# Prompt scores of a stick-breaking attention layer as three one-pass products of split queries and keys, and a cache ring of two places instead of three

## What is computed

```python
def sb_logits(q, k, sb_bias):
    z = jnp.einsum('bqhd,bkhd->bhqk', q, k).astype(jnp.float32) * SB_SCALE
    return z + sb_bias.astype(jnp.float32)[None, :, None, None]
# 8 heads x 64; prompt: strictly causal over 1024 keys in blocks of 128 queries
z = sb_logits(qb, k, sb_bias)
a = stick_breaking(z, valid)      # beta = sigmoid(z); beta * running product of (1 - beta)
o = jnp.einsum('bhqk,bkhd->bqhd', a, v)
# samples: the same against 16 gathered pages of 128 cached keys and values, and 4 new ones
k_past = cache_k[l][page_table].reshape(bs, -1, N_HEADS, HEAD_DIM)
v_past = cache_v[l][page_table].reshape(bs, -1, N_HEADS, HEAD_DIM)
```

## Time and profile before

| | |
|---|---|
| median of 3 runs | 1697.61 us (1697.18 to 1700.62) |
| profiled execution, its own time | 1698.21 us |
| its span, first to last instruction | 1696.4 us |
| TensorE busy | 1652.8 us, 97% |
| VectorE busy | 856.5 us, 50% |
| GpSimd busy | 600.9 us, 35% |
| ScalarE busy | 355.6 us, 21% |
| mean granted clock of TensorE | 0.997 |
| moved by DMA | 194.62 MB, 115 GB/s on average |

### The profile page before, as it was taken

The page is one execution under the profiler, slowest core; times in us unless marked ns, Lnnn a source line. Parts: engine busy times, 40 slices in busy tenths (PEclk is TensorE's granted clock), DMA queues, the critical chain, the costliest instruction groups (busy, mean ns, idle before and its releaser), DMA issues.

```text
span 1696.4 us, 29879 instructions
## 1 busy us (share of the span) xinstructions
PE 1652.8 (97%) x11976; PEld 1534.6 (90%) x11976; DVE 856.5 (50%) x1340; ACT 355.6 (21%) x668; POOL 600.9 (35%) x346
## 2 busy tenths in 40 slices
PE   6999999999999999999999899999999999999999
PEld 5898788878778788799999899999999999999998
DVE  5434264564553454338743866454544545454543
ACT  4233222222223222241111522020201011110200
POOL 0345043243344343313343243433433443343342
PEclk9999999999999999999999999999999999999999
DMA  9012256656656666425321011111111111111112
GB/s 378 29 48 100 103 175 224 224 200 212 200 181 232 211 228 226 161 103 203 127 102 50 26 50 50 39 50 50 47 41 50 50 38 50 50 42 47 50 38 103
DMA packets 71930, 194.62 MB, mean 115 GB/s; under 512 B 8017, under 2 KB 8146, under 8 KB 71794
## 3 DMA queue, kind: packets, MB, share of 16 engines
q1 hardware_dynamic: 67394, 178.62, 30.4%
q10 hardware_dynamic: 4400, 14.10, 2.2%
HBM read 174.26 MB, written 18.42 MB: 114 GB/s over the span
## 4 chain that ended last, share of the span: by engine, by line
PE 91%; DVE 3%; POOL 2%; DMA 1%; issue 1%; ACT 1%; SPq 1%; ACTq 0%; POOLq 0%; DVEq 0%
PE bank L648 77%; PE bank L795 2%; PE bank L770 2%; PE bank L783 2%; PE bank L819 2%; PE bank L843 1%; PE bank L678 1%; DMA pre<-in_weights 1%; POOL wl L585 1%; PE bank L734 1%; DVE sc L1557 1%; POOL wh L583 1%; DVE h2L L1525 1%; DMA ring<-in_cache_v 0%; SPq L492 0%
## 5 line engine op out<-in xcount | busy, mean ns | idle before, releaser
L583 POOL TENSOR_TENSOR wh<-raw,zero 128x1024 fp32r<-128x1024 f32 x86 | 163.4, 1900 | 658.2 <-PE bank L648 658.2
L585 POOL TENSOR_TENSOR wl<-raw,wh 128x1024 fp32r<-128x1024 f32 x114 | 281.9, 2473 | 88.6 <-ACT wh L1055 81.8
L648 PE MATMUL bank<-hH,wh 128*128 128x352 f32 x832 | 281.0, 338 | 0.7 <-POOL wl L585 0.7
L648 PE MATMUL bank<-hL,wh 128*128 128x352 f32 x832 | 267.4, 321 | 0.0
L648 PE MATMUL bank<-hH,wl 128*128 128x352 f32 x832 | 266.9, 321 | 0.0
L648 PE MATMUL bank<-h2H,wh 128*128 128x352 f32 x768 | 249.1, 324 | 1.8 <-DVE h2L L1525 0.9
L648 PE MATMUL bank<-hidH,wh 128*128 128x352 f32 x768 | 247.7, 323 | 0.0
L648 PE MATMUL bank<-h2H,wl 128*128 128x352 f32 x768 | 246.5, 321 | 0.0
L648 PE MATMUL bank<-h2L,wh 128*128 128x352 f32 x768 | 246.4, 321 | 0.0
L648 PE MATMUL bank<-hidH,wl 128*128 128x352 f32 x768 | 246.3, 321 | 0.0
L648 PE MATMUL bank<-hidL,wh 128*128 128x352 f32 x768 | 246.1, 320 | 0.0
(11 more groups left out here) (172 smaller groups left out, 2544.6 us busy)
## 6 DMA issues: line engine op xcount, KB each, us to landing
raw<-in_weights SPq DMA_DIRECT2D x152, 512.0 KB, 3.5
ring<-in_cache_k SPq DMA_DIRECT2D x128, 256.0 KB, 4.0
ring<-in_cache_v SPq DMA_DIRECT2D x128, 256.0 KB, 3.6
pre<-in_weights SPq DMA_DIRECT2D x16, 512.0 KB, 15.6
gate_scratch<-gt ACTq DMA_DIRECT2D x14, 528.0 KB, 3.4
act<-gate_scratch SPq DMA_DIRECT2D x14, 528.0 KB, 4.8
xt<-in_xT SPq DMA_DIRECT2D x8, 528.0 KB, 7.4
act<-in_xT SPq DMA_DIRECT2D x8, 528.0 KB, 4.6
```

The costliest lines, as they stand in the source:

```text
L583: mark(pool.tensor_tensor(wh[u % 2][:, :], src[:, :], zero[:, 0:1].to_broadcast([P, 1024]), ALU.add))
L585: pool.tensor_tensor(wl[u % 2][:, :], src[:, :], wh[u % 2][:, :].bitcast(F32), ALU.subtract)\
L648: mm = pe.matmul(out, x, y, start=n == 0, stop=n == end)
```

## The change

Queries and keys of a pair are split as the other operands are. Their high parts are written over them in place (`act8R` is `act8` under another type), their low parts go to a new tile `low_qk` for one pair at a time, which has the size of one place of the ring; the ring is two places long. `scores` makes three products for each head, alternating between the heads. The splits of pair 0 stand ahead of tick 0, those of pair p+1 in the last tick of pair p: `round_pair` (ScalarE, 2 activations of 128x1024), `low_pair` (VectorE, 2 subtractions), `high_pair` (ScalarE, 2 activations). The store of k, which reads the keys unsplit, is issued earlier, after the seventh copy of v, and `round_pair` waits for it.

```diff
-NKV = 3
+NKV = 2
...
         act8 = put("act8", [P, DB, T], F32)
+        act8R = put("act8R", [P, DB, T], F32R, at=act8_at)
...
+        low_qk = inw("low_qk", [P, 2, SEQ], F32R)
...
             def scores(k):
                 st = STEPS[k]
+                if k % (NSTEP // NPAIR) == 0:
+                    pe.wait_ge(S["pair_high"], 2 * st.p + 2)
                 for h in (0, 1):
-                    half = slice(HD * h, HD * h + HD)
...
-                    at = P * st.i + 512 * st.c
-                    pe.matmul(bank[2 + h][:, 0:st.n], act8[half, st.p, P * st.i:P * st.i + P],
-                              act8[half, NPAIR + st.p, at:at + st.n], start=True, stop=True).then_inc(S["z_done"], 1)
+                at = P * st.i + 512 * st.c
+                for n in range(3):
+                    for h in (0, 1):
+                        half = slice(HD * h, HD * h + HD)
+                        q = (low_qk[half, 0, :] if n == 1 else act8R[half, st.p, :])[:, P * st.i:P * st.i + P]
+                        keys = (low_qk[half, 1, :] if n == 2 else act8R[half, NPAIR + st.p, :])[:, at:at + st.n]
+                        mm = pe.matmul(bank[2 + h][:, 0:st.n], q, keys, start=n == 0, stop=n == 2)
...
# ScalarE, loop over the copies of v
+                if t == 6:
+                    act.wait_ge(S["qk_ready"], QK_N)
+                    for p in range(NPAIR):
+                        act.dma_start(a["kT"][:, p, :], act8[:, NPAIR + p, :]).then_inc(S["kout"], 16)
...
+            def round_pair(p):
+                act.wait_ge(S["kout"], 16 * NPAIR)
+                for x in (0, 1):
+                    act.activation(low_qk[:, x, :], act8[:, NPAIR * x + p, 0:SEQ], ACT.Copy).then_inc(S["pair_rounded"], 1)
+            def high_pair(p):
+                for x in (0, 1):
+                    act.wait_ge(S["pair_low"], 2 * p + x + 1)
+                    act.activation(act8R[:, NPAIR * x + p, 0:SEQ], act8[:, NPAIR * x + p, 0:SEQ], ACT.Copy)\
+                        .then_inc(S["pair_high"], 1)
+            round_pair(0)
+            high_pair(0)
             act.wait_ge(S["bank_act"], 9)
             act.dma_start(a["v"][0:SEQ].rearrange("(t p) c -> p t c", p=P), vsb[:, 0:8, :]).then_inc(S["vout"], 16)
...
# ScalarE, tick k
                     probability(k)
+                    if k in PAIR_ENDS:
+                        round_pair(STEPS[k].p + 1)
...
                     evict(DENSE_A[k], k)
                     split_high(DENSE_A[k])
+                if k in PAIR_ENDS:
+                    high_pair(STEPS[k].p + 1)
...
# VectorE, ahead of tick 0 (behind the copies to qb) and in tick k
+            def low_pair(p):
+                for x in (0, 1):
+                    dve.wait_ge(S["pair_rounded"], 2 * p + x + 1)
+                    tt(low_qk[:, x, :], act8[:, NPAIR * x + p, 0:SEQ], f(low_qk[:, x, :]), ALU.subtract).then_inc(S["pair_low"], 1)
+            low_pair(0)
...
                     keep_and_scan(k)
+                    if k in PAIR_ENDS:
+                        low_pair(STEPS[k].p + 1)
```

More of the change, by code:

```diff
@@ L205 @@
 NSTEP = len(STEPS)
+PAIR_ENDS = [_k for _k in range(NSTEP - 1) if STEPS[_k].p != STEPS[_k + 1].p]
 ITEMS = [(g, j) for g in (0, 1) for j in range(-1, PAGES)]
@@ L427, in program @@
             ada_in13 ada_in14 ada_in15 squares_added csig c_ready split_high squares_in_acc ada_copied ada_turned conv_first squares rms_done rstd dense_done bank_dve bank_act dve_step act_step
-            ada_done mods_done scaled h_hi h_lo h_sample qk_sq qk_sum qk_rs qk_ready kout vout
+            ada_done mods_done scaled h_hi h_lo h_sample qk_sq qk_sum qk_rs qk_ready kout vout pair_rounded pair_low pair_high
             z_done beta_done scan_done a_done at_done at_out0 at_out1 av_done o_out
@@ L768, in scores @@
                         pe.wait_ge(S["mods_done"], ADA_NTH[ADA_TURN_AT[k - 1]] + 1)
-                    at = P * st.i + 512 * st.c
-                    pe.matmul(bank[2 + h][:, 0:st.n], act8[half, st.p, P * st.i:P * st.i + P],
-                              act8[half, NPAIR + st.p, at:at + st.n], start=True, stop=True).then_inc(S["z_done"], 1)
+                at = P * st.i + 512 * st.c
[5 more added lines that the diff above has]
+                        mm = pe.matmul(bank[2 + h][:, 0:st.n], q, keys, start=n == 0, stop=n == 2)
+                        if n == 2:
+                            mm.then_inc(S["z_done"], 1)
             def turn(k):
@@ L1010, in _ @@
             act.preload_act_table_set("sigmoid_and_others")
-            act.wait_ge(S["qk_ready"], QK_N)
-            for p in range(NPAIR):
-                act.dma_start(a["kT"][:, p, :], act8[:, NPAIR + p, :]).then_inc(S["kout"], 16)
+            def round_pair(p):
[9 more added lines that the diff above has]
+            high_pair(0)
             act.wait_ge(S["bank_act"], 9)
```

## The result

The changed kernel takes 1739.79 us (1735.97 to 1741.02, 4 runs), the kernel before in the same comparison 1698.25 (1697.18 to 1700.62): a ratio of 1.024, with an interval from 1.0225 to 1.0254. It is slower, as said, but by 41.5 us and not by 22, and 1739.79 lies above the range. The profiled execution took 1738.93 us with a span of 1737.1, 40.7 more than before. TensorE's last step of the loop, step 47, starts 40.6 us later than in the trace of before: all of it is lost by then, and nothing is given back.

What follows compares the result with a forecast made beforehand. The prediction took TensorE, busy for 97% of the span, to bound the kernel. Its terms, - 4 + 7.3 + 2.2 + 17 = 22.5 us on the profiled 1698.2, gave 1720.7, stated as 1720 us, range 1707 to 1733.

Steps and rivals of the forecast that it cites:

- The products: Scores in every step: three one-pass products per head replace two passes, heads still side by side; 4 us gained.
- (a): Rival on the scores: weight loads of the three rounds are exposed, so scores gain nothing; 1724 us, chance 0.15.
- (b): Rival on the scores: the two heads no longer overlap, 22 us lost; 1746 us, chance 0.05 together with (e).
- (e): Rival on the scores: a float32r product of 64 rows still takes four passes, 61 us added; 1785 us, counted with (b).
- With 5.45 us a load the sum is 13.5: Lower case for the ring's late loads: each load takes 5.45 us instead of 6.0, so they cost 13.5 us.
- Ahead of tick 0: Before the loop: TensorE waits for the split of pair 0, then runs at half clock; 7.3 us lost, 5.6 without the clock.
- Tick 23: End of a pair: two high parts delay `turned`, for which `values` waits; 2.2 us lost, bounds 0 and 6.6.
- The ring: Cache loads with two places: late in ticks 5, 18, 29, 42 (13.2 us) and 13, 26, 37 (3.8); 17 us lost.
- I take 6.0: Time assumed for every cache load, from first issue to landing of its last page: 6.0 us.
- My bound of 24 us: Upper case for the ring: loads of 6.5 us cost 20.5, and some loads with little time left come in; 24 us.
- Rival (c): Rival on the ring: loads land faster with one under way, so it stays hidden; 1703 up to 1708 us, chance 0.09.
- Rival (d): Rival: faster than before, scores gain all 17.5 us, if the ring costs under 8; 1692 with 2, chance 0.03.

Runs made afterwards that it cites:

- products_only: Kernel before, three-place ring, with the three products all taking high parts, low parts not made, store of k issued earlier: 1694.61 us, 0.997 of the kernel before.
- split_early: Changed kernel with the splits of pair 0 made before v is finished, low parts in the ring's former first place: 1729.59 us, 1.0175 of the kernel before.
- ring_two_only: Kernel before with only two ring places used and no product changed: 1728.92 us, 1.0179 of the kernel before.
- filled_waits: Changed kernel with 12 unused matmuls ahead of the wait for v in ticks 5, 18, 26, 29 and 42: 1731.04 us, 1.0179 of the kernel before.
- loads_first: Changed kernel with SP's list reordered so cache loads stand ahead of weight tiles waiting for a split or `ada`: 1709.80 us, 1.0062 of the kernel before.
- changed_again: The changed kernel as it is, measured again on one chip with filled_waits: 1737.80 us, 1.0238 of the kernel before.
- all_three: Changed kernel with loads_first and split_early together, and high parts at pair ends made at other places: 1698.71 us, 0.9996 of the kernel before.
- products_filled: products_only with 11 unused matmuls in the wait of `values` in tick 34: 1694.23 us, 0.9974 of the kernel before.

## Why the prediction was right in sign and wrong in size

Taken from the starts of steps in the two traces, the 40.6 us are made up as follows; the predicted term stands in brackets.

- **The products: 5.3 us gained [4].** A step of 512, 384, 256 and 128 columns takes 0.89, 0.72, 0.55 and 0.48 us, where it took 1.06, 0.85, 0.63 and 0.42: 24 x 0.17 + 8 x 0.13 + 8 x 0.08 - 8 x 0.06. The model (0.11, three passes, 0.09) held, with the sizes 0.90, 0.74, 0.58 and 0.53. products_only, where nothing is paid for them in the ring, is 4.8 us faster, of which 1.6 is a wait of the earlier trace rows that is gone and to which a stretch at half clock (1.7) and a later start (1.1) stand opposed. So rivals (a) and (b) fall, and (e), whose working ended in a slip: 1698 and 61 are 1759, not the 1785 that stands there. (e) counted with (b) and moved neither the sum nor the range. The price of (a) was a slip too: two more loads of 0.11 make 1.12 us of 0.90, not 1.06, so that the scores would have lost some 5 us and (a) stood near 1729. And "With 5.45 us a load the sum is 13.5" should read 13.2.
- **Ahead of tick 0: 9.1 us lost [7.3].** `scores(0)` starts at 208.73, not at 207.8, as all steps of the chain run 0.7 to 1 us later than I put them. The half clock was priced at 1.7 and cost 2.5: the first group takes 5.8 us for 4.0, and the scores ahead of it 1.6 for 0.9. split_early gave the loss back, 7.9 at the start and 2.5 in tick 0; that is more than 9.1, as the wait for the first `probability` is gone there too.
- **Tick 23: 3.3 us lost [2.2].** The mechanism and its price are right: `turned` ends at 489.0, `values` waits 2.57 us where it waited 0.68, and the tick is 1.95 longer. The rest, 1.39 in tick 24, is a stretch at half clock behind that wait. The second group hides the splits in ticks 11 and 35, as said.
- **The ring: about 32 us lost [17].** This is the step that failed, "Together 13.2 + 3.8 = 17 us". Ten ticks (5, 6, 13, 17, 18, 26, 29, 37, 41, 42) are 30.7 us longer, some 32 without the products' gain in them. For 23.3 of it the data were late, and some 9 are the clock. (The 9.1 and 3.3 above hold 0.5 of the products' gain; without it - 5.3 + 9.3 + 3.6 + 32 is 39.6, and 1.0 of the 40.6 is left over, spread thinly.)

The ring's rule, that load i is issued where load i+1 stood, is borne out: v3 was forecast for tick 5 at 3.4 us short and was 2.73, v13, v21 and v31 came to 2.66, 3.36 and 3.91 for 3.0, 2.8 and 4.0. The four together are 12.7 for the forecast 13.2, tick 13 is 1.4 for 1.9. Both sizes that were off lie elsewhere.

The first is "I take 6.0" for a load. From first issue to TensorE's start v3, v13 and v31 took 5.8, 5.5 and 6.0, but v19 took 9.2 and cost 3.25 us (forecast 0.7), k28 took 8.3 and cost 2.87 (forecast 1.2) and k13 1.89 (no wait forecast). The landing of single DMAs of the changed kernel, from issue, in the windows 518 to 522 (v19) and 425 to 428 (v13):

```profile
DMA to landing us min/median/max: 6.2/6.3/6.6
...
DMA to landing us min/median/max: 3.2/3.5/3.8
```

The earlier trace rows gave 2.5 to 9.3 for one DMA. I used the median for every load, though a load that waits costs by its own landing and one that lands early gives nothing back: with such a spread, the mean of the shortfalls is more than the shortfall of the mean. My bound of 24 us "with 6.5" would have held the 23.3.

The trace of before had more to give than a spread. I read each load's issue from the load that stood one place later, and could have read its landing there as well. The load in v19's place, k21, before (SP's queue, its DMAs, and TensorE's first use of v19):

```profile
496.93 2.69 SPq L484 DMA_DIRECT2D ring<-in_cache_k  x4
DMA to landing us min/median/max: 6.2/6.3/7.8
...
502.23 1.04 PE L843 MATMUL bank<-ring,sAT 128*32 128x512 f32 x8
```

It took 9.85 us to its last landing, the loads in the places of k28 and k13 took 8.1 and 8.3, and those of v3, v13 and v31 5.9, 5.5 and 5.7. The shortfalls by these are 4.6, 2.7 and 1.8 us for v19, k28 and k13, where the waits were 3.25, 2.87 and 1.89. Over all loads this working gives 29 us, too much where one late load follows another, but it names the places that I missed.

The second was in no bound at all. I priced the half clock ahead of tick 0, from a wait of 4.0 us, and did not ask the same of the ring's waits, of which I had listed four of 2.8 to 4.0 us. ring_two_only has 8.1 us beyond its waits, filled_waits is 6.8 faster with the data as late as ever, and loads_first won 30 by removing 20.2 us of waits. That the clock takes a part is thus shown; that it is the whole of what lies beyond the waits is argued from the sums. The size allows it: the six stretches next to late loads last 20.5 us together and can cost up to 10.2. With it and the 23.3 the sum is - 4 + 7.3 + 2.2 + 23.3 + 9 = 37.8; the misses of the other terms (- 1.3, + 1.8, + 1.1) make it 39.4 of the 40.6.

Rival (c) held that loads land faster when fewer are under way. A DMA landed after 3.7 us at the median instead of 3.9, which is next to nothing, and (c)'s 1703 is 37 us away. Rival (d) needed a ring that costs little, and products_only shows what it would then give: with the ring whole and no low parts made, 4.8 us, not 17.5.

## What to carry to other kernels

Before taking a buffer from a ring, read in the queue what each load stands behind: in a queue that works in order, the load inherits its neighbours' waits, and moving the neighbour (30 us here) can be worth as much as the buffer (29.5). Price every new wait of the busiest engine twice, once for its length and once for the clock, which may fall next to it, and take the landing time of a load from the load that holds its place in the queue now, not from the median of all. A product that gains 0.17 us a step has to be weighed against the one-off splits and the memory that it needs, since these decided the sign.

## What the hardware did that I had not expected

- The granted clock halved behind waits of TensorE of 1.9 to 3.9 us, for 3.4 us and sometimes 6.8. In ticks 5 and 23 it did so 1.4 and 1.6 us after work had begun again, in ticks 29, 37 and 42 already in the last 0.2 to 0.5 us of the wait. It did not do so behind every such wait, nor in every execution: in changed_again tick 26 waits 2.53 us at the same place and the clock stays at 1.00 behind it, where the first profile of the same program, with a wait of 3.25, has 0.50. A wait of 1.77 us left the clock at 1.00 in the kernel before, and had 0.50 behind it in all_three. What decides it between waits as like as these, the runs leave open.
- In the profiled executions of four kernels the clock stayed up behind each wait that was filled with unused matmuls, but stretches at half clock stand elsewhere: at tick 23 in products_filled, and in filled_waits at 518.8, behind a wait for keys of 2.15 us in tick 26 that was not filled.
- Some places in the queue are slow whoever holds them. v19's four issues took 2.94 us and its DMAs 6.2 to 6.6 to land, and k21 before was as slow in that place; v3's took 1.90 and 3.2 to 4.1. More traffic is not the reason that shows: the DMA engines were less busy around v19 than around v3 (last two columns, DMA share and GB/s). Nor does a slow landing need slow issues: k28's took 1.88 us, and it landed 8.1 us after the first. The cause stays open.

```profile
271.00:277.00 6.00, 3.94 (x66) 3.19 (x64) 1.94 (x6) 1.43 (x3) 1.23 (x3) 1.00 0.94 342
518.00:524.00 6.00, 5.80 (x65) 5.30 (x63) 4.01 (x8) 1.60 (x4) 3.34 (x2) 1.00 0.87 285
```

- The two stores of v took 0.39 and 0.60 us of ScalarE's queue where they took 1.24 and 2.36 before, for the same bytes, 5 us later.
